# The order of VectorE and ScalarE work in a gated-delta scan and at its head ends, sums in three PSUM banks, constants in two loads, squares three tiles ahead

## The reference, cut to what matters

```python
xn = rms_norm(h, mix_norm_w)
proj = xn @ w_in                       # gate_b, gate_c, u, qkv, z, a, b
y_a = rms_norm(gate_b * conv3(gate_c * u), per group of 64)          # "mix"
q, k, v = split(silu(conv4(qkv)));  q, k = l2_normalize(q), l2_normalize(k)
# per head and chunk of tokens, with decay from cumsum(g):
#   (I + lower(beta k k^T decay)) [u | w] = [beta v | beta k exp(g)]
def step(S, chunk):
    v_new = u_c - w_c @ S
    o_c   = qg_c @ S + intra_c @ v_new
    return S * a_c + kd_c.T @ v_new, o_c
o = rms_norm(o) * silu(z)              # "o"
h = h + concat(y_a, o) @ w_out
h = h + hierarchical_moe(rms_norm(h)); out = rms_norm(h)[16:]
```

## Time and profile before

| | us |
|---|---|
| median of 3 runs | 1517.64 (1516.69 to 1518.26) |
| the profiled execution, its own time | 1517.29 |
| its span, first to last instruction | 1515.5 |
| PE busy | 1319.4 (87%) |
| DVE busy | 933.1 (62%) |
| ACT busy | 722.9 (48%) |
| POOL busy | 157.5 (10%) |

### The profile page before, as it was taken

The page is one execution under the profiler, slowest core; times in us unless marked ns, Lnnn a source line. Parts: engine busy times, 40 slices in busy tenths (PEclk is TensorE's granted clock), DMA queues, the critical chain, the costliest instruction groups (busy, mean ns, idle before and its releaser), DMA issues.

```text
span 1515.5 us, 20621 instructions
## 1 busy us (share of the span) xinstructions
PE 1319.4 (87%) x7574; PEld 1141.4 (75%) x7574; DVE 933.1 (62%) x1178; ACT 722.9 (48%) x927; POOL 157.5 (10%) x145
## 2 busy tenths in 40 slices
PE   4989997999899989869995289999999999999960
PEld 4989897988798879647774268887888888888840
DVE  5753455345533553333224678888888888888837
ACT  5441224133413341242223067777777777777723
POOL 0010111011101110111110011111111111111000
PEclk9999999999999999759996589999999999999985
DMA  7100010001010100234331279999999999999848
GB/s 195 43 15 29 15 43 16 29 20 37 16 29 27 30 15 1 112 111 117 100 95 40 97 277 364 363 379 379 381 391 382 377 384 367 383 375 373 336 174 332
DMA packets 37024, 274.49 MB, mean 181 GB/s; under 512 B 8040, under 2 KB 8168, under 8 KB 23656
## 3 DMA queue, kind: packets, MB, share of 16 engines
q1 hardware_dynamic: 27032, 250.88, 45.1%
q0 software_dynamic: 9216, 17.06, 2.9%
q10 hardware_dynamic: 720, 5.73, 1.1%
HBM read 260.67 MB, written 29.49 MB: 191 GB/s over the span
## 4 chain that ended last, share of the span: by engine, by line
PE 61%; DVE 15%; ACT 11%; issue 10%; DMA 2%; ACTq 0%; DVEq 0%; POOLq 0%; POOL 0%
PE bank L1124 6%; PE bank L1126 6%; PE bank L1125 6%; PE bank L510 6%; PE bank L512 6%; PE bank L511 6%; DVE w_lo L743 5%; ACT w_hi L622 4%; PE bank L1245 3%; PE bank L1243 3%; PE bank L434 3%; PE bank L435 2%; PE bank L436 2%; ACT xgT_hi L640 2%; DVE arena L896 1%
## 5 line engine op out<-in xcount | busy, mean ns | idle before, releaser
L743 DVE TENSOR_TENSOR w_lo<-w_raw,w_hi 128x2048 fp32r<-128x2048 f32 x192 | 433.4, 2286 | 68.4 <-ACT w_hi L622 68.4
L622 ACT ACTIVATE w_hi<-w_raw 128x2048 fp32r<-128x2048 f32 x192 | 357.2, 1916 | 19.7 <-PE bank L512 13.5
L1124 PE MATMUL bank<-xn_hi,p_hi 128*128 128x346 f32 (+1 forms) x672 | 232.0, 345 | 3.5 <-DVE p_lo L1525 3.5
L1126 PE MATMUL bank<-xn_hi,p_lo 128*128 128x346 f32 (+1 forms) x672 | 219.1, 326 | 0.0
L1125 PE MATMUL bank<-xn_lo,p_hi 128*128 128x346 f32 (+1 forms) x672 | 219.0, 326 | 0.0
L510 PE MATMUL bank<-w_hi,xgT_hi 128*128 128x512 f32 x512 | 206.6, 403 | 2.9 <-DVE xgT_lo L889 2.9
L512 PE MATMUL bank<-w_hi,xgT_lo 128*128 128x512 f32 x512 | 200.9, 392 | 0.0
L511 PE MATMUL bank<-w_lo,xgT_hi 128*128 128x512 f32 x512 | 200.6, 392 | 0.0
L1124 PEld LDWEIGHTS bank<-xn_hi,p_hi 128*128 128x128 f32 x672 | 129.9, 193 | 5.2 <-DVE p_lo L1525 3.2
L1125 PEld LDWEIGHTS bank<-xn_lo,p_hi 128*128 128x128 f32 x672 | 129.7, 193 | 0.7 <-issue 0.7
L1126 PEld LDWEIGHTS bank<-xn_hi,p_lo 128*128 128x128 f32 x672 | 129.2, 192 | 0.0
(11 more groups left out here) (237 smaller groups left out, 2057.9 us busy)
## 6 DMA issues: line engine op xcount, KB each, us to landing
w_raw<-in_w_down SPq DMA_DIRECT2D x32, 2048.0 KB, 9.8
w_raw<-in_w_gate SPq DMA_DIRECT2D x31, 2048.0 KB, 10.5
w_raw<-in_w_up SPq DMA_DIRECT2D x31, 2048.0 KB
p_raw<-in_w_tiles SPq DMA_DIRECT2D x28, 512.0 KB, 3.5
arena<-in_tokens SPq DMA_DIRECT2D x20, 416.0 KB
arena<-y_rows SPq DMA_DIRECT2D x8, 1024.0 KB, 12.1
h_rows<-arena SPq DMA_DIRECT2D x10, 416.0 KB
xn_rows<-arena SPq DMA_DIRECT2D x10, 416.0 KB
```

Source lines behind the costliest of these rows:

```text
L622: nc.scalar.activation(w_hi[m][:, half], wraw[m][:, half], ACT.Copy).then_inc(hi_done[m], 1)
L743: nc.vector.tensor_tensor(w_lo[m][:, half], wraw[m][:, half], w_hi[m][:, half].bitcast(F32), ALU.subtract).then_inc(lo_done[m], 1)
L1124: nc.tensor.matmul(out[:, 0:n], p_hi[slot][:, k, :], hi, start=(k == 0), stop=False)
L1126: m = nc.tensor.matmul(out[:, 0:n], p_lo[slot][:, k, :], hi, start=False, stop=(k == KD - 1))
```

## The change

It has five parts. (1) The constants are reordered, so that `ident`, `eps`, `ob` and `sel` (138 columns) come first and are loaded alone; `mix_w` (now 104 rows) is loaded second, `par` third, the other constants last; PE and ACT's first logarithm wait for the first part only, DVE's taps and ACT's `wab` copy for the rest. (2) ACT does the norms of tokens 0, 1 and 2 in its first turn and `token_norm(t+2)` in turn t. (3) The sums use banks 6, 7 and 2, without a wait between the pieces, but "mix" waits for DVE to have taken GB and "o" for ACT to have taken V. (4) The splits of GC and UU move from the start and the head ends into the head that uses them; in the start only Z's split is left, with its high part behind the first silu. (5) In the scan DVE does one convolution step (or V's `lo_part`) between the residual and the wait for `ods_done` and one behind the output, and ACT does its `hi_part`s and the silu of q behind the `vn` copy, ahead of the wait for `o_done`.

```diff
 _at = 0
-for _n, _w in [("ident", 128), ("ones", 128), ("bones", 128), ("incl", C), ("strict", C), ("lev", LEVELS * C),
-               ("iota", 128), ("tok", NC), ("dst", 2 * NC), ("r4", NG), ("r8", EPG), ("eps", 1), ("ob", 1), ("sel", 8)]:
+for _n, _w in [("ident", 128), ("eps", 1), ("ob", 1), ("sel", 8), ("ones", 128), ("bones", 128), ("incl", C),
+               ("strict", C), ("lev", LEVELS * C), ("iota", 128), ("tok", NC), ("dst", 2 * NC), ("r4", NG), ("r8", EPG)]:
     CONST[_n] = (_at, _w)
...
 NCONST = _at
+NFIRST = CONST["ones"][0]
...
-        s_const, s_wout, s_ffw = sem("const_loaded"), sem("w_out_loaded"), sem("ffw_loaded")
+        s_first, s_const, s_wout, s_ffw = sem("first_loaded"), sem("const_loaded"), sem("w_out_loaded"), sem("ffw_loaded")
         x_loaded = [sem(f"x_loaded{s}") for s in range(NC)]
...
+        SUM_BANK = [6, 7, 2]
+
         def sums(h, name, pieces=3):
...
             for pc, (o, n) in enumerate(PIECE):
-                b = 6 + (SUMS.index(name) + pc) % 2
-                if pc == 2:
-                    pe.wait_ge(sum_act, sums(h, name, 1))
-                nc.tensor.matmul(bank[b][:, 0:n], mat, src[:, o:o + n], start=True, stop=True).then_inc(sum_done, 1)
+                nc.tensor.matmul(bank[SUM_BANK[pc]][:, 0:n], mat, src[:, o:o + n], start=True, stop=True).then_inc(sum_done, 1)
...
         def _(pe):
-            pe.wait_ge(s_const, 32)
+            pe.wait_ge(s_first, 16)
...
                         pe.wait_ge(sq_done, h + 1)
+                        pe.wait_ge(proj_dve, by_dve(h, GB))
                         sum_pieces(pe, h, "mix", sq[0], bones)
...
                 pe.wait_ge(osum_done, h * NC + NC)
+                if not last:
+                    pe.wait_ge(proj_act, by_act(h, V))
                 sum_pieces(pe, h, "o", sq[1], ones)
...
         def _(act):
-            act.dma_start(const_sb, consts).then_inc(s_const, 16)
+            act.dma_start(const_sb[:, 0:NFIRST], consts[:, 0:NFIRST]).then_inc(s_first, 16)
+            act.dma_start(mixrow[0:C, :], mix_w[0:C, :]).then_inc(s_mix, 16)
             act.dma_start(par_sb, par).then_inc(s_const, 16)
-            act.dma_start(mixrow, mix_w).then_inc(s_mix, 16)
+            act.dma_start(const_sb[:, NFIRST:NCONST], consts[:, NFIRST:NCONST]).then_inc(s_const, 16)
             nc.scalar.preload_act_table_set("natural_log_exp_and_others")
...
                 if t == 0:
-                    act.wait_ge(s_const, 32)
+                    act.wait_ge(s_first, 16)
                 act.wait_ge(ss_done, 2 * t + 1)
...
             for t in range(NC + 1):
-                if t < NC:
-                    token_norm(t)
+                for tt in (range(3) if t == 0 else range(t + 2, min(t + 3, NC))):
+                    token_norm(tt)
                 if t:
...
                 if t == 5:
+                    act.wait_ge(s_const, 32)
                     nc.scalar.activation(wab_hl[:, :, 0:8], wab, ACT.Copy).then_inc(wab_done, 1)
...
                 first_piece(n)
-            hi_part(1, 2)
...
                     act.wait_ge(sum_done, sums(h, name, pc + 1))
-                    nc.scalar.activation(sq[buf][:, o:o + n], bank[6 + (buf + pc) % 2][:, 0:n], ACT.Ln,
+                    nc.scalar.activation(sq[buf][:, o:o + n], bank[SUM_BANK[pc]][:, 0:n], ACT.Ln,
                                          scale=scale, bias=shift).then_inc(sum_act, 1)
...
                 silu(dst, s)
-            hi_part(2, 2)
-            hi_part(0, 2)
+                if s == 0:
+                    hi_part(0, 2)
             for pc, (o, n) in enumerate(PIECE):
...
                     nc.scalar.activation(dT[0:C, gsl(g), :], dT[0:C, gsl(g), :], ACT.Exp).then_inc(dexp_done, 1)
+                hi_part(1, use(h, GC))
                 nc.scalar.activation(sq[1], cv[0], ACT.Square, scale=0.128).then_inc(cq_done, 1)
...
                 gc_piece(0)
+                hi_part(2, use(h, UU))
                 hi_part(0, use(h, GB))
...
                     nc.scalar.activation(vn_sb[0:C, :], bank[4][0:C, 0:128], ACT.Copy).then_inc(vn_done, 1)
+                    if not last and c == 1:
+                        hi_part(0, use(h + 1, Z))
+                    if not last and c == 4:
+                        hi_part(SLOT[V], use(h, V))
+                    if not last and c == 6:
+                        act.wait_ge(conv_step, h * 15 + CONV0 + 7)
+                        silu(cv[0], 0)
                     act.wait_ge(o_done, h * NC + c + 1)
...
                         evac_raw(c % 3, (c // 3) % 2)
-                    if not last and c == 1:
-                        hi_part(0, use(h + 1, Z))
-                    if not last and c == 4:
-                        hi_part(SLOT[V], use(h, V))
-                    if not last and c == 6:
-                        act.wait_ge(conv_step, h * 15 + CONV0 + 7)
-                        silu(cv[0], 0)
                 if not last:
...
                     silu(cv[2], 2)
-                    hi_part(2, use(h + 1, UU))
-                    hi_part(1, use(h + 1, GC))
                 log_exp_tables()
...
+            dve.wait_ge(s_const, 32)
             nc.vector.tensor_copy(taps, taps_all[:, 0:16]).then_inc(taps_done, 1)
...
                     m.then_inc(conv_step, 1)
-            lo_part(1, 2)
-            lo_part(2, 2)
             lo_part(0, 2)
...
                 grp(h, "vtr")
+                lo_part(1, use(h, GC))
                 for g in range(3):
...
-                lo_part(0, use(h, GB))
+                lo_part(2, use(h, UU))
                 grp(h, "z1")
...
                 u_piece(0)
+                lo_part(0, use(h, GB))
                 grp(h, "rz2")
...
                                                    bv[0:C, c, :], ALU.mult, ALU.add).then_inc(r_done, 1)
+                    if not last and c in (3, 4, 6, 7):
+                        if c in (3, 6):
+                            dve.wait_ge(proj_act, by_act(h, Q if c == 3 else K))
+                        next(todo[c // 6])
+                    if not last and c == 5:
+                        lo_part(SLOT[V], use(h, V))
                     dve.wait_ge(ods_done, h * NC + c + 1)
...
                                                    ALU.mult, ALU.mult).then_inc(o_done, 1)
-                    if not last and c in (2, 5):
-                        lo_part(0 if c == 2 else SLOT[V], use(h + 1, Z) if c == 2 else use(h, V))
+                    if not last and c == 2:
+                        lo_part(0, use(h + 1, Z))
                     if c == 1:
...
                     if not last and c in (3, 4, 6, 7):
-                        if c in (3, 6):
-                            dve.wait_ge(proj_act, by_act(h, Q if c == 3 else K))
-                        for _ in range(2):
-                            next(todo[c // 6])
+                        next(todo[c // 6])
                 if not last:
...
                     k_sums(h + 1)
-                    lo_part(2, use(h + 1, UU))
-                    lo_part(1, use(h + 1, GC))
```

## The result

The changed kernel takes 1506.95 us (median of 4 runs, 1503.36 to 1508.1) where the kernel before, run beside it, takes 1517.95 (1516.69 to 1519.38). The ratio is 0.9924, 95% interval 0.9908 to 0.994. So it is faster, clear of the noise, but by 11 us (0.8%) and not by 31.6: the prediction of 1485.7 was wrong, and 1506.95 lies outside its range of 1477 to 1498.

The account below looks back on a forecast made before the run. PE was taken to bound the heads, with time to win only where it idles or runs slow. 24.0 + 8.2 + 1.3 - 7.6 + 4.8 + 0.9 = 31.6 us off 1517.3 gave 1485.7, range 1477 to 1498.

Parts of the forecast that it names:

- Part 1: Three head ends: sums run back to back, next fill at full clock, "grow" 8.0 us earlier each, 24.0 in all.
- Part 3: Splits now inside all four heads: a cost of 1.9 us per head, 7.6 in all, between 3.6 and 9.2.
- Part 2: "mix" sums in four heads: waits for logarithms go, 8.2 us; half clock behind the third head's "mix" goes, 1.3.
- part 4: Scan of three heads: late chunks lose their extra time, 1.6 us per scan, 4.8 in all, bounds 0 and 5.4.
- part 5: The start: projections 3.6 us later, but fewer splits ahead of the first fill; net gain 0.9, bounds -0.8 and +1.9.
- X: In the start, the time ACT can begin the square of token 4: forecast 22 us.
- Rival 1: Head ends gain less, through DVE's lag at "vtr" or a clock fall: 3.9 x 3, total 1497; chance 0.17.
- DVE's lag: Behind head ends, DVE takes up "grow" 2.6 us after PE: costs nothing by the sum, up to 1.7 per end.
- Rival 2: The start gains: token 4's rows come faster, projections up to 5 us before their old time; 1477, half 1481; chance 0.12.
- Rival 3: At head ends another wait holds the sums as long as the logarithm did: 24.0 goes, 1509.7 stays; chance 0.03.
- Rival 4: PE stays at half clock through scans of heads with a successor: 28 x 3 = 84 us lost, about 1570; chance 0.02.

Follow-up runs that it names:

- Experiment 1: Changed kernel with PE's wait for the third "o" logarithm moved behind the next head's "grow": 1497.73 us, ratio 0.9853.
- experiment 5: Changed kernel with PE's loop over the first three heads written out, so no jump between heads: 1498.76 us, ratio 0.9873.
- experiment 6: Changed kernel with ACT's high parts of UU and GB moved ahead of the first GC piece: 1494.92 us, ratio 0.9833.
- Experiment 7: Experiment 1 plus POOL's product for qg held until PE's third transpose of "ttr1": 1487.88 us, ratio 0.9799.
- experiment 4: Changed kernel with DVE's order in the scan put back as before, ACT's kept: 1509.41 us, ratio 0.9949.
- Experiment 3: Changed kernel with each token's norm in its own turn, not turns ahead: 1502.84 us, ratio 0.9891.
- experiment 8: Changed kernel with the edits of experiments 1, 3, 6 and 7 together: 1471.93 us, ratio 0.9693.

## Why the prediction was wrong

- **Part 1 is the step that failed: "plus about 0.3 for the loop's turn".** The logarithms, the sums and the fill came as worked out. But the turn costs 4.2 us where PE has nothing queued. The sum took it for 0.3 and cited no row; the nearest, the 0.48 us of the earlier trace rows, is what was left of it under the slow fill. That is 3.9 us at two ends. With the half clock behind it (2.6 each), 13.3 of the missing 21.0 us are here: 24.0 - (16.0 - 5.3). The third end, with no jump, won 7.3. Experiment 1 takes the wait away from ahead of the jump, experiment 5 takes the jump away, and both give back the idle time and the clock.
- The price of the table load, 1.28 us by the row, held: in the kernel after it is 1.28 again, with the silu ending 0.02 ahead of it and the next instruction 0.01 behind it. The 2.66 us that the Trainium skill ("ScalarE: Activation LUTs", What ACT_TABLE_LOAD costs) counts for a switch are not seen here.
- **Part 3 was right in place and mis-sized, 15.8 for 7.6.** The wait at z1 (0.94 more in each head) was right, but the sum had no term for the clock: its fall behind 1.95 idle us cost 4.8 in the profiled run, and with the idle time gone in experiment 6 it doesn't fall there. The split of GC was costed at DVE's 1.22 us, from rows where no POOL instruction held it up. Begun while POOL's product runs it takes up to 3.12, and 3.43 in experiment 5. In experiment 1 it takes 4.29 in the last head, where it begins under POOL's masks and the product follows them. Experiment 7 moved the product alone and had 9.9 us back. The round ahead of "ttr0", counted at nothing, took the last 0.9. The Trainium skill ("SBUF — State Buffer", Who interferes with whom) says that a VectorE instruction with two SBUF inputs is blocked by a GpSimd instruction that reads SBUF, for the whole of it, if that one came first. By that rule the trace agrees: both inputs of the split are in SBUF, and in all twenty cases in the profiles where it was stretched beside the product it ends 1.07 to 1.09 us behind it.
- **Part 2** (10.9 for 9.5), **part 4** (5.5 for 4.8; mainly DVE's order, by experiment 4) and **part 5** (1.0 for 0.9, X = 21.96 for 22, turn_x(4) 3.7 later for 3.6) held. In part 2 the "mix" sums gave 9.5 for 8.2 and the clock 1.4 for 1.3. Experiment 3 shows that part 5's squares ahead were themselves a loss: the gate rows come 5.2 us earlier without them, and the total is 4.1 lower. X by the bytes alone would have been 0.4 less than 22, but as the 22 rests on an estimated 1 us, 21.96 doesn't tell the two apart. Nor does the share of 0.84 in the earlier trace rows that was read as 13 of 16: it is above 0.81.
- The stages behind the heads took 854.25 against 852.55. They were taken as unchanged. In the ten profiles of this study they take 852.5 to 854.6, and in experiment 4, whose code there is the changed kernel's, 852.6; so the 1.7 us is scatter between runs as far as these profiles show.
- **Rivals.** Rival 1 came nearest: something else did become the bound at the head ends and the clock fell in spite of the forecast, but DVE's lag had no part in it (with "grow" early in experiment 1, "vtr" follows it in 5.6), the idle time was not under 1 us but 4.7, and it was priced at 3.9 an end where two ends lost 6.3. It reached only 1497, since the splits' 8.2 were in no rival with it. Rivals 2, 3 and 4 fell: turn_x(4) came later and not sooner, the sums waited for nothing long, and the clock over a whole head is 0.97 to 0.99.

The range failed for the same reason. Its bounds were those of durations seen in rows; a cost that lay hidden beneath the very wait that the change removes had no row and got no bound.

## What to carry to other kernels

Before a long wait of TensorE is removed, ask what else ran beneath it: here a loop's jump of 3.7 us, which shows only as idle time ended by "issue" once nothing covers it. Place the last wait of a loop's body behind the first matmuls of the next turn, so that the jump runs while matmuls are queued. And price moved work by what the other engines do at its new place: a pass of VectorE over two SBUF operands beside one of GpSimd, or 1 us more of idle time ahead of a row of matmuls, cost here two and a half to three and a half times their own length in the worst heads, and nothing in others. Compare such effects by stretches of the profile: the clock alone shifts a total by several us from run to run.

## What the runs showed of the hardware

- A backward jump of PE's loop over a head (about a thousand matmuls) takes 3.3 to 3.8 us in all nine profiles with the loop, while one packet of about 16 KB of instructions (124 GB/s in a slice of 0.13 us) lands inside it; one that falls through takes 0.08, and one of the short loops behind the heads 0.21 to 0.24. The Trainium skill ("Advanced Engine Details and Errata", Control Flow Timing) gives about 108 ns for a compare-and-branch: the fall-through lies a little below this, the short loops' jumps at twice of it, and the long loop's nowhere near. That the long jump waits for instructions to be loaded again is argued from that packet, and from its absence in the short loops; no run varied the length of the loop.
- The granted clock fell to 0.50 behind the 1.95 us of idle time at z1 in 10 of the 24 heads of the six profiles that have it (three of four in the changed kernel, none of four in experiment 4), and in none of the 8 heads with 1.01 us. After the 4.4 to 4.9 us of idle time around the bare jump it fell 8 times in 8, after 0.8 to 1.35 us there (experiments 1, 7 and 8) never in 6.
- DVE's split, 1.21 us alone, was stretched to between 1.3 and 4.3 us where POOL was at work first. With three masks and the product of POOL back to back, the split got in behind one of the masks in experiment 7 (without the product) and only behind all of them in experiment 1; what decides this is not shown. It holds the other way round too: in the kernel before, a split of DVE (309.52 to 310.73) begins just ahead of POOL's product at L1799 and takes its 1.21, and the product takes 2.83, where in the last head, without a split beside it, it takes 1.92. DVE's three products of gk, with one operand in a bank, took 1.36 us with POOL's masks beside them for the first 0.6 (experiment 7) and 1.36 without POOL (the last head of the changed kernel).

```profile
309.68 2.83 POOL L1799 TENSOR_TENSOR arena<-arena 128x1040 f32<-128x1040 f32 x1 [59.22 <-DVE arena L1696]
```
